# Another order for the input projections of a second mixer, and a one-column exponential after the logarithm

## What is computed

```python
h = rms_norm_2(x, norm_g)
z = h @ w_in          # split into fq fk fv ff f_gate glu_in c_gate
                      #   nq nkc nvc nks nvs nkw nvw n_gl n_gate
o_a = fox_attention(fq, fk, fv, ff + fox_b) * silu(f_gate)   # log decay: a running sum of log sigmoid(ff)
o_b = conformer_conv(glu_in, ...) * silu(c_gate)             # 31 taps over time, layer norm
o_c = nsa_attention(nq, nkc, nvc, nks, nvs, nkw, nvw, n_gl, ...) * silu(n_gate)
#     nsa: compressed blocks of nkc, nvc through a small network (w1: 1024 to 256 columns, gelu, w2),
#     selected blocks (nks, nvs), a window (nkw, nvw); mixed by sigmoid(n_gl)
x = x + concat(o_a, o_b, o_c) @ w_out
```

## Time and profile before

| | |
|---|---|
| median of 3 runs | 1596.47 us (1594.84 to 1596.88) |
| the profiled execution's own time | 1595.83 us |
| its span | 1594.0 us |
| TensorE busy | 1580.5 us, 99% |
| VectorE, ScalarE, GpSimd busy | 60%, 50%, 10% |
| DMA | 269.60 MB, mean 169 GB/s |
| mixers of the second block | from about 1257 us to the end |

### The profile page before, as it was taken

How to read it: one execution, slowest core, us unless ns; L and a number is a source line. 1 busy time by engine, 2 the same in 40 slices (tenths; PEclk the granted TensorE clock), 3 DMA queues, 4 the chain that set the end, 5 groups by cost and what they waited for, 6 DMA issues and landing times.

```text
span 1594.0 us, 22882 instructions
## 1 busy us (share of the span) xinstructions
PE 1580.5 (99%) x8772; PEld 1368.8 (86%) x8772; DVE 955.8 (60%) x1454; ACT 801.4 (50%) x1358; POOL 167.3 (10%) x187
## 2 busy tenths in 40 slices
PE   9999999999999999999999999999999999999998
PEld 7888899988888888888889988888888888889896
DVE  5555475544765554655456554575554678777876
ACT  6444464455364444544455455445444546553654
POOL 0000022211300000000021221121000301010000
PEclk9999999999999999999999999999999999999999
DMA  7666456443455554655546444446566454244521
GB/s 258 206 208 207 148 182 199 133 147 130 154 181 190 190 186 159 211 185 185 189 157 202 147 146 134 131 157 212 193 212 201 150 189 154 87 145 155 193 88 65
DMA packets 76718, 269.60 MB, mean 169 GB/s; under 512 B 8512, under 2 KB 9792, under 8 KB 76608
## 3 DMA queue, kind: packets, MB, share of 16 engines
q1 hardware_dynamic: 76320, 267.35, 51.5%
q10 hardware_dynamic: 288, 0.79, 0.1%
HBM read 267.06 MB, written 1.05 MB: 168 GB/s over the span
## 4 chain that ended last, share of the span: by engine, by line
PE 95%; ACT 1%; DVE 1%; DMA 1%; issue 1%; POOL 1%; POOLq 0%; SPq 0%; ACTq 0%
PE bank L1453 26%; PE bank L1455 26%; PE bank L1454 26%; PE bank L1459 5%; PE bank L1578 2%; PE bank L1593 2%; PE bank L1710 2%; PE bank L1516 1%; PE bank L1520 1%; PE bank L1512 1%; DMA raw<-W 1%; PE bank L1682 0%; PE bank L1687 0%; PE bank L1686 0%; DVE wlo L2302 0%
## 5 line engine op out<-in xcount | busy, mean ns | idle before, releaser
L2302 DVE TENSOR_TENSOR wlo<-raw,whi 128x1024 fp32r<-128x1024 f32 (+5 forms) x472 | 571.4, 1220 | 398.8 <-ACT whi L1988 369.2
L1988 ACT ACTIVATE whi<-raw 128x1024 fp32r<-128x1024 f32 (+4 forms) x500 | 508.5, 1029 | 414.4 <-PE bank L1455 378.1
L1453 PE MATMUL bank<-whi,hh 128*128 128x512 f32 (+3 forms) x1120 | 433.8, 387 | 0.0
L1455 PE MATMUL bank<-whi,hl 128*128 128x512 f32 (+3 forms) x1120 | 425.2, 380 | 0.0
L1454 PE MATMUL bank<-wlo,hh 128*128 128x512 f32 (+3 forms) x1120 | 424.5, 379 | 0.0
L1455 PEld LDWEIGHTS bank<-whi,hl 128*128 128x128 f32 x1120 | 210.5, 188 | 38.4
L1454 PEld LDWEIGHTS bank<-wlo,hh 128*128 128x128 f32 x1120 | 210.8, 188 | 36.1
L1453 PEld LDWEIGHTS bank<-whi,hh 128*128 128x128 f32 x1120 | 210.7, 188 | 35.7
L1453 PE MATMUL bank<-hh,whi 128*128 128x256 f32 x480 | 142.9, 298 | 0.0
L1453 PE MATMUL bank<-whi,gh 128*128 128x512 f32 x352 | 139.3, 396 | 0.0
L1455 PE MATMUL bank<-whi,gl 128*128 128x512 f32 x352 | 137.9, 392 | 0.0
(11 more groups left out here) (326 smaller groups left out, 1903.3 us busy)
## 6 DMA issues: line engine op xcount, KB each, us to landing
raw<-W SPq DMA_DIRECT2D x463, 512.0 KB, 3.4
raw<-W SPq DMA_DIRECT2D x26, 384.0 KB, 3.6
raw<-W SPq DMA_DIRECT2D x8, 416.0 KB, 3.0
tab<-tab SPq DMA_DIRECT2D x6, 384.0 KB, 4.0
raw<-W SPq DMA_DIRECT2D x4, 426.0 KB, 3.0
raw<-W SPq DMA_DIRECT2D x6, 192.0 KB, 2.8
x<-x_in SPq DMA_DIRECT2D x2, 512.0 KB, 6.8
tab<-gains SPq DMA_DIRECT2D x2, 512.0 KB, 4.3
```

Of the source, the lines that this page charges most:

```text
L1453: e.matmul(dst, ah, bh, start=start, stop=False)
L1455: return e.matmul(dst, al, bh, start=False, stop=stop)
L1988: return e.activation(dst, src, ACT.Copy)
L2302: return e.tensor_tensor(dst, src, hi.bitcast(F), ALU.subtract)
```

## The change

The projections of the second mixer are now made in the order `nq`, `n3`, `g0`, `g1`, `nkv`, `ci`, in both layers, and the weight blocks lie in DRAM in that order. While `g0` is projected, one step of gates and decay is issued at each of its four pauses; three pauses of `ci` are empty, and the fourth issues the scan. While `nkv` is projected, three taps instead of two are issued per pause. The sequence after the projections is now `ffmmtdmftfm` (f transposes, m main stream, t taps, d decay). Behind the logarithm and the sum stands `m2_exp_table`, an exponential of one column whose result nobody reads; it makes ScalarE load the exponential's table there. The order of attention pairs is written as a string of letters and is the same as before.

```diff
--- before.py
+++ after.py
@@ -14,6 +14,11 @@
+ROW_ORDER = ('nq', 'n3', 'g0', 'g1', 'nkv', 'ci')
+DECAY_STEPS = {'nq': 0, 'g0': 1, 'g1': 0, 'nkv': 0, 'ci': 1}
+TAP_STEPS = {'nkv': 3, 'ci': 0, 'n3': 2, 'nq': 0}
+UNIT_ORDER = 'aaabbaccccbbffggdddd'
+FIRST_STEPS = 'ffmmtdmftfm'
@@ -84,13 +89,16 @@
-        rows("nq", "w_in_2", l, range(8), [(NQ + h * 64, 64) for h in NQ_HEADS], 2)
-        for c in [GA, GB, GA + 128, GB + 128]:
-            cols("col2", "w_in_2", l, 8, c)
-        for c in [NKC, NVC]:
-            cols("col2", "w_in_2", l, 8, c)
-        rows("nkv", "w_in_2", l, range(8), [(NKS, 128), (NKW, 128), (NVS, 128), (NVW, 128)], 2)
-        rows("n3", "w_in_2", l, range(8), [(FV, 256), (FFG, 4), (NGL, 24)], 3)
+        for z in ROW_ORDER:
+            if z == "nq":
+                rows("nq", "w_in_2", l, range(8), [(NQ + h * 64, 64) for h in NQ_HEADS], 2)
+            elif z == "nkv":
+                rows("nkv", "w_in_2", l, range(8), [(NKS, 128), (NKW, 128), (NVS, 128), (NVW, 128)], 2)
+            elif z == "n3":
+                rows("n3", "w_in_2", l, range(8), [(FV, 256), (FFG, 4), (NGL, 24)], 3)
+            else:
+                for c in {"g0": [GA, GB], "g1": [GA + 128, GB + 128], "ci": [NKC, NVC]}[z]:
+                    cols("col2", "w_in_2", l, 8, c)
@@ -800,7 +808,7 @@
-                if (key, t) == ("nq", 0):
+                if (key, t) == (ROW_ORDER[0], 0):
@@ -812,9 +820,6 @@
-
-        yield from self.row_group("nq", 8, 2, 512, "h", norm.n, take_rows("nq", 512), 4, norm, self.WB)
-        xnf = list(self.xn_free)
@@ -825,22 +830,21 @@
-        for n in range(2):
-            yield from self.col_pair("col2", norm.n, take_glu(n), self.WB)
-        self.do("m2_glu_tanh", l)
-        yield from self.col_pair("col2", norm.n, lambda use: self.do("m2_cmp_in", l, norm, use, base), self.WB)
-        self.do("m2_blocks", l, base)
-        taps = conv()
-
-        def with_taps(gen, n):
-            for w in gen:
-                for _ in range(n):
-                    next(taps, None)
-                yield w
-
-        yield from with_taps(self.row_group("nkv", 8, 2, 512, "h", norm.n, take_rows("nkv", 512), ring=self.WB), 2)
-        self.do("m2_rotate", l, xnf)
-        yield from with_taps(self.row_group("n3", 8, 3, 284, "h", norm.n, take_rows("n3", 284), ring=self.WB), 1)
+
+        def block(z):
+            if z in ("g0", "g1"):
+                yield from self.col_pair("col2", norm.n, take_glu(int(z[1])), self.WB)
+                if z == "g1":
+                    self.do("m2_glu_tanh", l)
+            elif z == "ci":
+                yield from self.col_pair("col2", norm.n, lambda use: self.do("m2_cmp_in", l, norm, use, base), self.WB)
+                self.do("m2_blocks", l, base)
+            else:
+                per, w = {"nq": (2, 512), "nkv": (2, 512), "n3": (3, 284)}[z]
+                if z == ROW_ORDER[0]:
+                    yield from self.row_group(z, 8, per, w, "h", norm.n, take_rows(z, w), 3 if z == "n3" else 4, norm, self.WB)
+                else:
+                    yield from self.row_group(z, 8, per, w, "h", norm.n, take_rows(z, w), ring=self.WB)
@@ -852,6 +856,8 @@
+            self.do("m2_exp_table")
+            yield
@@ -1094,8 +1100,28 @@
-        for z in (taps, first, decays, main, decays, main, taps, first, first, decays, taps, main, main, decays):
-            next(z)
+        taps, done = None, []
+        for z in ROW_ORDER:
+            for w in block(z):
+                if z == ROW_ORDER[0]:
+                    yield w
+                    continue
+                if "n3" in done:
+                    for _ in range(DECAY_STEPS.get(z, 0)):
+                        next(decays, None)
+                if "g1" in done:
+                    taps = taps or conv()
+                    for _ in range(TAP_STEPS.get(z, 0)):
+                        next(taps, None)
+                yield w
+            if z == ROW_ORDER[0]:
+                xnf = list(self.xn_free)
+            done.append(z)
+            if {"nq", "nkv"} <= set(done) and z in ("nq", "nkv"):
+                self.do("m2_rotate", l, xnf)
+        taps = taps or conv()
+        for z in FIRST_STEPS:
+            next({"d": decays, "f": first, "m": main, "t": taps}[z], None)
@@ -1124,9 +1150,9 @@
-        near, far = nsa_pairs(0, 1), nsa_pairs(0, 2)
-        todo = iter_chain(limited(near, 3), limited(far, 2), near, nsa_pairs(1, 1), far, fox_pairs(0), fox_pairs(1),
-                          nsa_pairs(1, 2))
+        gens = {"a": nsa_pairs(0, 1), "b": nsa_pairs(0, 2), "c": nsa_pairs(1, 1), "f": fox_pairs(0), "g": fox_pairs(1),
+                "d": nsa_pairs(1, 2)}
+        todo = (next(gens[z]) for z in UNIT_ORDER)
@@ -2149,6 +2175,9 @@
+    def m2_exp_table():
+        e.activation(T.sm[:, 396:397], T.half[:, 0:1], ACT.Exp).then_inc(*q.tell("scal"))
+
```

More of the change, by code:

```diff
@@ L2283, in scalar @@
         m1_turn_latent, m1_q, m1_v, m1_turn_heads, m1_exp, m1_turn, m1_turn_group, m1_gate, m1_turn_merged, mixer1_end,
-        m2_rows, m2_glu_tanh, m2_branch_gates, m2_decay_in, m2_decay_log, m2_decay_scan, m2_decay_b, m2_turn_n, m2_fqk,
+        m2_rows, m2_glu_tanh, m2_branch_gates, m2_decay_in, m2_decay_log, m2_exp_table, m2_decay_scan, m2_decay_b, m2_turn_n, m2_fqk,
         m2_fg, m2_cg_tanh, m2_ng, m2_ln_square, m2_silu_in, m2_silu, m2_conv_gate, m2_scores, m2_turn, m2_gelu_square,
```

## The result

The changed kernel takes **1599.36 us as the median of nine runs (1596.98 to 1601.66)**, the kernel before 1595.11 us as the median of nine runs on the same chip. The medians are 4.25 us apart. Over all runs the ratio is 1.0022, with a 95% interval of 1.0013 to 1.0031: slower by 0.2%, by 2.1 to 4.9 us. The profiled execution of the change took 1598.67 us with a span of 1596.9 us. That is 2.84 us more than the profiled execution before, and I account for it first.

A forecast was written before the change was run, and what follows sets the result against it. TensorE, 99% busy, bounds the kernel; its late transposes hang on the first `cmp` block's start. +3.0 us over both layers and -0.3 for row scales made +2.7 on 1595.83, 1598.5; as a median 1599.1 us, range 1595.0 to 1601.8.

The forecast's parts named there:

- Keys and values last: In each layer the first `cmp` block waits for its inputs `bl`, starting 3.5 us after the projections end, against 0.53.
- The stream: Five `cmp` weight blocks loaded in sequence; first block to split `whi` takes 11.58 us in layer 0, 11.18 in layer 1.
- `fb` out of the way: On ScalarE three `fb` no longer stand between `whi` and the copy: 3.54 us to the late transposes becomes 2.05.
- E to T: Projections' end (E) to the second attention pair's transposes (T): 17.15 and 16.75 us against 15.65 and 15.24, 3.0 us more.
- Spreading: Layer 0's row scales: the second transpose, which waits 0.24 us for GpSimd, comes some 6 us later; -0.3 us.
- Table loads: ScalarE's logarithm and exponential loads, 1.28 us each, move to the time of `g0`; counted as nothing at either place.
- So T hangs on the start of the first `cmp` block: The late transposes wait for the five-block DMA stream, 9.1 and 8.6 us, which begins when the first `cmp` block frees a buffer.
- This idle time also swallows whatever comes up to 1.5 us later: TensorE's idle time before the late transposes, 1.95 and 1.55 us, hides transposes, scores or exponentials up to 1.5 us later.
- three half-speed stretches: TensorE at 1.2 GHz for 3.4 us from about 1320.2, 1368.0 and 1487.5 us, each costing about 1.7 us.
- second rival: The late transposes don't wait for the stream: 1592.3 to 1595.7 us, perhaps without both half-speed spells there; chance 0.12.
- The half-speed stretch on the new idle time: First rival: half speed at the first `cmp` block, up to 0.95 us per layer; 1600.0 or 1601.0 us, chance 0.2.
- third rival: The wait before the first `cmp` block isn't there: `bl` is in time, the `fb` gain is won; 1595.4 us, chance 0.13.

The follow-up runs named there:

- r1: The changed kernel with `ci` ahead of `nkv` again and three `cmp` blocks first behind the projections; ratio 0.9999 to the kernel before.
- r7: The changed kernel without the one-column exponential; 1598.40 us against 1599.36.
- r8: The kernel before with only the one-column exponential added behind the sum of the decay; 2.0 us more in the median, 2.4 by the ratio.
- r4: The changed kernel with the last four `cmp` blocks of each layer loading 256 of 1024 columns; 2.8 us less in the median.
- r6: The kernel before with the last four `cmp` blocks of each layer loading 256 of 1024 columns; median moved by about 1 us, interval holds no change.
- r2: The changed kernel with the scan and decay steps moved behind the first `cmp` block; median 1601.34 us.
- r3: The changed kernel with six pauses between the sign step and the four `fb`; median 1600.32 us.

## Why the prediction was right, and where it wasn't

The median, 1599.36 us, is 0.3 us above the forecast 1599.1 and inside the range. That closeness is partly luck. The forecast stood on a kernel before of 1596.47 us, the median of three runs; nine runs gave 1595.11. As a difference 2.6 us were forecast and 4.25 us measured, so the direction and the place were right and the size was short. Step by step:

- **Keys and values last: right.** E + 3.63 for the first block against E + 3.5, with idle times of 0.98 us ahead of the transposes (`cuml` as releaser) and 0.75 us ahead of the block, against 1.2 and 0.8. `xT` 1.73, `cuml` 0.35 net, and half of the four `bl`. These four took 2.80 us instead of the 2.20 of the earlier trace rows; that is the 0.1 us. r1 shows that this wait is what the change costs.
- **The stream: right in size, a little short.** From the first block to `whi` it took 11.78 us in layer 0 and 11.58 in layer 1, against 11.58 and 11.18 in the sum; 297 and 308 GB/s against 295 and 314.
- **`fb` out of the way: right.** 2.08 us from `whi` to the copy's reader against 2.05.
- **E to T: right in kind, 0.9 us short.** 17.49 and 17.29 us against 17.15 and 16.75, so 3.9 us more in two layers, not 3.0. Of the 0.9 us the stream has 0.6 and the first block 0.3.
- **Spreading: right.** The second transpose of the row scales no longer waits; the two stand as one row without a stop at 1281.99. It brought 0.5 us against 0.3.
- **Table loads: right here, for a reason I hadn't given.** r7 confirms the nothing in the change. But "since T waits for the DMA and not for the first exponentials" is wrong of the kernel before, as r8 shows.
- **"So T hangs on the start of the first `cmp` block": half right.** It is so in the change (r4), but in the kernel before a second chain ended as late (r6). The profile had it: the third `fb` and the pair of exponentials stood right there, and the split (ScalarE, kernel before, layer 0) waited hardly at all:
```profile
1316.75 1.06 ACT L1988 ACTIVATE whi<-raw 128x1024 fp32r<-128x1024 f32 x1 [0.19 <-DMA raw<-W]
```
  It says that taking the DMA's lateness away wins 0.19 us before the next thing is late. In layer 1 the same wait is 0.75 us, and r6 won 0.6 us at T there. This did no harm to the sum, because the change removed that chain and lengthened the other.
- **"This idle time also swallows whatever comes up to 1.5 us later": right as far as T.** TensorE now stops for the sixth block (0.56 us; 0.41 and 0.38 for two blocks in layer 1), and the stop at T, 1.52 and 1.23 us in place of the 1.95 and 1.55 of the sum, is smaller by about as much; T itself is set by `whi`. But the sum ended at T and had nothing for what comes behind. That is 0.67 us in layer 1, where a stop of 1.25 us stands behind T, and nothing in layer 0.
- **What hid the miss: the clock.** The sum kept the three half-speed stretches of the earlier trace rows at 1.7 us each. The profiled execution of the change has none of them. The one at 1368 was worth 1.67 us, as priced; the two behind T were worth nothing at G, as the account shows, and the second rival's "up to 2 x 1.7 us" for them wouldn't have come. So the 2.84 us are +3.9 at T, +0.6 from T to G, +0.5 at the start in work that is the same, less 0.5 for the row scales and 1.7 for the stretch at 1368. The forecast of 2.7 us is nearly this number because errors of opposite sign cancel. The medians, 4.25 us apart, show more of the true cost than the two profiles do.
- **The rivals.** The half-speed stretch on the new idle time didn't happen. r2, where the idle time is one piece, has it in both layers, which fits the argument "two parts, with transposes between". But single pieces of 1.92 us (r6) and 2.21 us (r3, layer 1) passed without one, so the argument isn't proven. The stream was what T waited for (second rival out). The wait was where I put it (third rival out). The Trainium skill (DMA: Bandwidth & Descriptors, Specifications) has about 358 GB/s as a core's limit. The means of the stream, 297 and 308 GB/s, stay below it, while single slices go above it: the earlier trace rows reach 419, not 382 as the prediction says. By the page's figure T would have been TensorE's own, and it wasn't.

**Left open:** why the profiled execution of the change escapes the half-speed stretch at 1368, where TensorE makes the same products of 32 columns without idling in both kernels; why T to G takes anything from 41.2 to 42.8 us in the layers of r1 to r4 and r6 to r8; and how much of the stops behind T is order and how much is supply. No kernel of these beats the one before by more than the measurement can tell.

## What to carry to other kernels

Moving a projection to the end of its group takes the cover from whatever is made out of it: price the work of the other engine between the last projection and its first reader, here 3.6 us, against every chain that starts there. A wait that is short in the profile (0.19 us here) is a sign of a second chain close behind, and taking the first away wins about that and no more. And price a slow stretch or a stop by the distance between two fixed marks, not by its own length: here a half-speed stretch of 3.4 us in open work cost 1.7 us, and the same stretch ahead of copies that come late anyway cost nothing.

## What I hadn't expected of the hardware

A half-speed stretch followed one idle piece of 2.31 us in both layers of r2, idle pieces of 1.95 and 2.17 us in the kernel before, and one of 1.72 us in r3, but not pieces of 0.98, 0.75 and 1.52 us in the change. Idling isn't its only occasion, nor does it always bring one: r8 has a stop of 1.91 us at T with a half-speed stretch behind it and one of 1.92 us without, r6 one of 1.92 us and r3 one of 2.21 us without, and the one at 1368 of the earlier trace rows comes in work without a stop and is absent from the same work in the change. And what such a stretch costs depends on where it falls: 1.67 us at 1368, nothing at G behind T, and 1.6 us at T where it lies on the blocks that start the stream (the longer one in layer 1 of r2 against that in layer 0).
